# Expert loops of a two-layer mixture-of-experts kernel: the third product of each expert is issued behind the first two of the next

## What is computed

```
def run(args):
    xb, e = args
    return (jax.nn.silu(xb @ w1[e]) * (xb @ w3[e])) @ w2[e]
```

## Time and profile before

| | |
|---|---|
| median of 3 runs | 2323.3 us (2322.07 to 2324.07) |
| span of the profiled execution | 2330.8 us |
| PE busy | 2074.1 us (89%) |
| DVE, ACT, POOL busy | 787.4, 468.8, 189.3 us |
| moved in all | 640.95 MB, mean 275 GB/s |
| weight tiles of the experts | 192 of 2 MB |
| expert loop of layer 0, first product to last | 353.8 to 851.0 us |
| expert loop of layer 1, first product to last | 1095.4 to 1582.0 us |

### The profile page before, as it was taken

One profiled execution on the slowest core, in us unless ns is written; L12 is line 12 of the kernel. 1 busy time (PEld: TensorE's weight loads), 2 busy tenths in 40 slices (PEclk: granted clock), 3 DMA queues, 4 the chain that ended last, 5 costly groups with the idle time before them and its releaser, 6 DMA issues.

```text
span 2330.8 us, 30150 instructions
## 1 busy us (share of the span) xinstructions
PE 2074.1 (89%) x11971; PEld 1230.5 (53%) x11972; DVE 787.4 (34%) x1836; ACT 468.8 (20%) x1059; POOL 189.3 (8%) x240
## 2 busy tenths in 40 slices
PE   6998998889877889989877877798999999999998
PEld 4566475344444435757433433343775575775574
DVE  1355673111111116646111111114456413457413
ACT  2142112111111112411211111111123113123122
POOL 1000011111111110001111111111000000000000
PEclk9999999999999999979999999999999999999999
DMA  9236559999999993566999999997343233343230
GB/s 371 109 127 256 233 181 399 424 408 407 393 426 426 426 396 124 232 278 247 420 425 425 425 425 425 426 387 276 145 163 127 100 142 139 145 164 113 104 145 19
DMA packets 62872, 640.95 MB, mean 275 GB/s; under 512 B 15868, under 2 KB 16420, under 8 KB 24240
## 3 DMA queue, kind: packets, MB, share of 16 engines
q1 hardware_dynamic: 41728, 588.39, 61.4%
q0 software_dynamic: 19984, 44.74, 5.4%
q10 hardware_dynamic: 1056, 6.37, 0.7%
HBM read 622.50 MB, written 44.17 MB: 286 GB/s over the span
## 4 chain that ended last, share of the span: by engine, by line
PE 68%; DMA 21%; DVE 5%; ACT 3%; issue 2%; SPq 0%; POOL 0%; DVEq 0%; POOLq 0%; ACTq 0%
PE ps L854 17%; DMA ring<-in_moe 16%; PE ps L988 10%; PE ps L506 8%; PE ps L1002 6%; PE ps L1101 5%; PE ps L494 3%; PE ps L683 3%; PE ps L528 3%; PE ps L1173 2%; PE ps L860 2%; DMA ring<-in_denseA 2%; PE ps L759 2%; DVE scr L1767 2%; PE ps L857 1%
## 5 line engine op out<-in xcount | busy, mean ns | idle before, releaser
L854 PE MATMUL ps<-ring,scr 128*64 128x256 f32 (+1 forms) x4800 | 695.3, 445 | 102.2 <-DMA ring<-in_moe 53.4
L854 PEld LDWEIGHTS ps<-ring,scr 128*64 128x64 f32 x4800 | 348.2, 141 | 429.0 <-issue 170.2
L988 PE MATMUL ps<-ring,hT 128*128 128x512 f32 (+1 forms) x576 | 245.0, 577 | 2.0 <-ACT hT L1493 2.0
L1767 DVE TENSOR_TENSOR scr<-ps,scr 128x512 f32<-128x512 f32 (+3 forms) x98 | 54.7, 558 | 482.8 <-PE ps L854 401.5
L2429 DVE COPY scr<-ps 128x1024 f32<-128x1024 f32 x64 | 78.4, 1225 | 380.7 <-PE ps L854 345.7
L506 PE MATMUL ps<-ring,hT 128*128 128x512 f32 (+1 forms) x512 | 203.0, 555 | 4.1 <-ACT hT L1515 3.2
L1391 POOL DMA_INDIRECT ys_scratch<-scr,ytab x128 | 124.7, 974 | 838.2 <-DVE scr L2429 802.4
L988 PEld LDWEIGHTS ps<-ring,hT 128*128 128x128 f32 x576 | 107.3, 192 | 114.6 <-issue 109.5
L1463 ACT ACTIVATE scr<-ps 128x256 f32<-128x256 f32 (+2 forms) x168 | 71.3, 436 | 406.6 <-PE ps L494 406.5
L506 PEld LDWEIGHTS ps<-ring,hT 128*128 128x128 f32 x512 | 98.5, 195 | 98.9 <-issue 91.6
L1002 PE MATMUL ps<-hT,ring 128*128 128x256 f32 x640 | 145.5, 382 | 0.0
(11 more groups left out here) (331 smaller groups left out, 2059.6 us busy)
## 6 DMA issues: line engine op xcount, KB each, us to landing
ring<-in_moe SPq DMA_DIRECT2D x192, 2048.0 KB
ring<-in_denseB SPq DMA_DIRECT2D x48, 2048.0 KB
ring<-in_denseA SPq DMA_DIRECT2D x36, 2048.0 KB
scr<-ys_scratch POOLq DMA_DIRECT2D x6, 1024.0 KB, 7.6
modB<-mod_scratch POOLq DMA_DIRECT2D x10, 512.0 KB, 11.4
ring<-kv_scratch SPq DMA_DIRECT2D x2, 2048.0 KB
tok_scratch<-hb POOLq DMA_DIRECT2D x6, 512.0 KB, 2.9
memT_scratch<-modB ACTq DMA_DIRECT2D x2, 1024.0 KB, 6.7
```

The lines of the kernel that those rows point to most:

```text
L854: last = mm(out, lhs(c)[:, 0:64], w(c)[:, half * q:half * (q + 1)], start=(c == 0), stop=(c == n - 1))
L988: last = mm(T["open"][:, 0:cols], hT16[:, c, t * P:(t + 1) * P], w[:, c, 0:cols], start=(c == 0), stop=(c == DC - 1))
L1767: return V.tensor_tensor(out, a, b, op)
```

## The change

PE's function `expert` is taken apart into `up` (one of the first two products), `turn_gated` (the four transposes) and `down` (the third product). The new order is: first product of expert u, transposes of u - 1, second product of u, third product of u - 1. Each part has its own branch on narrow or wide. The third product of the last expert stands alone behind the loop. ACT and DVE follow the same order. SP loads the tiles in the new order (`place`, `in_order`, `tile_of`): w1 and w3 of expert 0, w1 and w3 of expert 1, w2 of expert 0, w1 and w3 of expert 2, w2 of expert 1, and so on. The two first products of an expert now lie in neighbouring banks (2p and 2p + 1), the output table moves from bank 3 to bank 7, the token blocks use banks 4 and 5 but for block 1 (2 and 3), and `down` waits by itself until the output before it is copied out.

```
+    def place(u, k):
+
+        if k == 2:
+            return 3 * u + 4 if u < E - 1 else 3 * E - 1
+        return 3 * u - 1 + k if u > 0 else k
+
...
-                released[baseM[l] + 3 * b + k] = (s, blocks_before[l] + b + 1)
+                released[baseM[l] + place(b, k)] = (s, blocks_before[l] + b + 1)
...
+            def up(i, u, k, flag):
...
+                def work(is_wide):
+                    w = moe_tile(i, G0 + (3 * u - 1 + k if u > 0 or type(i) is not int else k))
+                    products(2 * p + k, lambda c: w[:, c, :], DC, 512, lambda c: xgT[:, p, c, :],
+                             is_wide).then_inc((m_h1, m_h3)[k], 1)
...
+            def turn_gated(i, u, flag):
+
+                p = u % 2
+                pe.wait_ge(m_g, i * UNROLL + (B0 + u + 1))
...
+            def down(i, u, flag, q):
+
+                p = u % 2
+                pe.wait_ge(m_ge, i * UNROLL + (B0 + u + 1))
+                if B0 + u > 0 or type(i) is not int:
+                    pe.wait_ge(m_ye, i * UNROLL + (B0 + u))
...
+            now = flag_of(0, 0)
+            pe.wait_ge(m_xc, B0 + l + 1)
+            pe.wait_ge(cols_dve, l + 1)
+            up(0, 0, 0, now)
+            turn_block(1)
+            up(0, 0, 1, now)
+            output_table()
+            for u in range(1, UNROLL):
+                before, now = now, flag_of(0, u)
+                beside = blocks_beside(l, u)
+                pe.wait_ge(m_xc, B0 + l + u + 1)
+                up(0, u, 0, now)
+                turn_gated(0, u - 1, before)
+                up(0, u, 1, now)
...
+                if u == 1:
+                    pe.wait_ge(dest_ready, l + 1)
+                down(0, u - 1, before, G0 + 3 * u + 1)
...
             with pe.Fori(1, E // UNROLL) as i:
+                now = flag_of(i, -1)
                 for u in range(UNROLL):
-                    expert(u, i, False)
+                    before, now = now, flag_of(i, u)
+                    pe.wait_ge(m_xc, i * UNROLL + (B0 + l + u + 1))
+                    up(i, u, 0, now)
+                    turn_gated(i, u - 1, before)
+                    up(i, u, 1, now)
+                    down(i, u - 1, before, G0 + 3 * u + 1)
+            now = flag_of(0, E - 1)
+            turn_gated(0, E - 1, now)
+            down(0, E - 1, now, G0 + 3 * E - 1)
...
-            dense(lambda i: d["moe"][l][3 * EPG * (i // 3) + i % 3], 3 * UNROLL, G0)
+            dense(lambda i: d["moe"][l][tile_of(*in_order[i])], 3 * UNROLL - 1, G0)
...
-                    q = j - RING
-                    s = (m_h1, m_h3, m_y)[q % 3]
-                    sp_.wait_ge(s, i * UNROLL + (B0 + UNROLL + q // 3 + 1))
...
+                    m, k = divmod(j - RING, 3)
+                    sp_.wait_ge((m_h1, m_h3, m_y)[k], i * UNROLL + (B0 + UNROLL + m + (k < 2)))
...
+            dense(lambda i: d["moe"][l][tile_of(E - 1, 2)], 1, G0 + 3 * E - 1)
...
             with act.Fori(1, E // UNROLL) as i:
                 for u in range(UNROLL):
...
+                    silu_of(u % 2, i * UNROLL + (B0 + u))
+                    gated_out((u - 1) % 2, i * UNROLL + (B0 + u - 1))
+                    expert_tokens((u + 1) % 2, bass.ds(i * UNROLL + u + 1, 1), m_xc)
+            gated_out((E - 1) % 2, B0 + E - 1)
...
             for part in range(7):
                 table_part(part)
...
+                if part == 2:
+                    take_block(1)
...
             with dve.Fori(1, E // UNROLL) as i:
                 for u in range(UNROLL):
                     gated(u % 2, i * UNROLL + (B0 + u))
-                    outputs(u % 2, i * UNROLL + (B0 + u), i * 64 + (32 * ((B0 + u) // 2) + 16))
+                    outputs((u - 1) % 2, i * UNROLL + (B0 + u - 1), i * 64 + (32 * ((B0 + u - 1) // 2) + 16))
+            outputs_of(E - 1)
```

More of the change, by code:

```diff
@@ L414, in program, with tile_of @@
             for k, s in enumerate((m_h1, m_h3, m_y)):
-                released[baseM[l] + 3 * b + k] = (s, blocks_before[l] + b + 1)
+                released[baseM[l] + place(b, k)] = (s, blocks_before[l] + b + 1)
+    in_order = sorted(((u, k) for u in range(E) for k in range(3)), key=lambda at: place(*at))
+    def tile_of(u, k):
+        return 3 * (EPG * (u % NG) + u // NG) + k
     def blocks_beside(l, u):
@@ L422, in block_banks @@
     def block_banks(k):
[L424 to L425 removed]
+        return (2, 3) if k == 1 else (4, 5)
     def par_a(l):
@@ L831, in output_table @@
                 pe.wait_ge(tab_in, l + 1)
-                table = ps[:, 3, :]
+                table = ps[:, 7, :]
                 pairs = [(k, t) for k in range(2) for t in range(nt)]
@@ L863, in _ @@
             pe.wait_ge(plan_ready, l + 1)
-            def expert(u, i, peeled):
-                p = u % 2
[L869 to L903, removed]
@@ new lines, in moe_tile, with flag_of, either @@
+            def moe_tile(i, q):
+                pe.wait_ge(ring_full[q % RING], i * 48 + 16 * (q // RING + 1))
+                return ring[:, q % RING, :, :]
+            def flag_of(i, u):
+                return pe.value_load(wide[0:1, bass.ds(i * UNROLL + u, 1)], min_val=0, max_val=1)
+            def either(flag, work):
+                with pe.If(flag > 0):
+                    work(True)
+                with pe.Else():
+                    work(False)
+            def up(i, u, k, flag):
+                p = u % 2
+                def work(is_wide):
+                    w = moe_tile(i, G0 + (3 * u - 1 + k if u > 0 or type(i) is not int else k))
+                    products(2 * p + k, lambda c: w[:, c, :], DC, 512, lambda c: xgT[:, p, c, :],
+                             is_wide).then_inc((m_h1, m_h3)[k], 1)
+                either(flag, work)
@@ L904, in down, with work @@
+            def turn_gated(i, u, flag):
+                p = u % 2
+                pe.wait_ge(m_g, i * UNROLL + (B0 + u + 1))
+                def work(is_wide):
                     for c in range(4):
-                        bank, o = p + 2 * (c // 2), (c % 2) * P
-                        if flag:
+                        bank, o = 2 * p + c // 2, (c % 2) * P
+                        if is_wide:
                             last = nc.tensor.transpose(ps[:, bank, o:o + P],
@@ new lines, in down, with work @@
+            def down(i, u, flag, q):
[3 more added lines that the diff above has]
+                    pe.wait_ge(m_ye, i * UNROLL + (B0 + u))
+                def work(is_wide):
+                    w = moe_tile(i, q).rearrange("p (k n) x -> p k (n x)", n=2)
+                    products(6, lambda c: w[:, c, :], 4, D, lambda c: gT[:, p, c, :],
+                             is_wide).then_inc(m_y, 1)
+                either(flag, work)
@@ L1613, in _, with silu_of @@
             act.wait_ge(plan_ready, l + 1)
[L1614 to L1622, removed]
+            def silu_of(p, b):
+                act.wait_ge(m_h1, b + 1)
+                A(eb[:, p, :], ps[:, 2 * p, :], ACT.Silu).then_inc(m_e, 1)
+            silu_of(0, B0)
+            take_block(1)
+            blocks_taken(2)
+            expert_tokens(1, slice(1, 2), m_xc)
+            for u in range(1, UNROLL):
+                silu_of(u % 2, B0 + u)
+                gated_out((u - 1) % 2, B0 + u - 1)
+                beside = blocks_beside(l, u)
+                if beside:
+                    take_block(beside[0])
+                blocks_taken(min(u + 2, SLOT_BLOCKS[l]))
+                expert_tokens((u + 1) % 2, slice(u + 1, u + 2), m_xc)
+                if beside:
+                    take_block(beside[1])
+            blocks_taken(SLOT_BLOCKS[l])
             with act.Fori(1, E // UNROLL) as i:
                 for u in range(UNROLL):
[L1625 to L1631, removed]
+                    silu_of(u % 2, i * UNROLL + (B0 + u))
+                    gated_out((u - 1) % 2, i * UNROLL + (B0 + u - 1))
+                    expert_tokens((u + 1) % 2, bass.ds(i * UNROLL + u + 1, 1), m_xc)
+            gated_out((E - 1) % 2, B0 + E - 1)
             o = ov[l]
@@ L2436, in _, with outputs_of @@
                 table_part(part)
-            for u in range(UNROLL):
-                gated(u % 2, B0 + u)
[L2439 to L2444, removed]
+                if part == 2:
+                    take_block(1)
+            def outputs_of(u):
+                outputs(u % 2, B0 + u, 32 * ((B0 + u) // 2) + 16)
+            gated(0, B0)
+            rows_of_outputs()
+            for u in range(1, UNROLL):
+                gated(u % 2, B0 + u)
+                beside = blocks_beside(l, u)
+                if beside:
+                    take_block(beside[0])
+                outputs_of(u - 1)
+                if beside:
+                    take_block(beside[1])
+                if u == 2:
                     gate_values()
```

19 lines of the change are left out of this document (14 added, 5 removed).

## The result

| | before | changed |
|---|---|---|
| median of 6 runs, side by side | 2323.47 us (2322.07 to 2335.21) | 2309.24 us (2307.67 to 2312.99) |
| ratio, 95% interval | | 0.9939 (0.9921 to 0.9958) |
| profiled execution, span | 2330.8 us | 2308.0 us |
| PE busy | 2074.1 us | 2038.9 us |
| loop of layer 0, first product to first `MEM_V` product | 498.91 us | 489.91 us |

The kernel is faster by 14.2 us (0.6%). Forecast were 17.0 us and 2306.3 us. The line between loops and the rest is drawn at two rows of PE's timeline that both kernels have, the first product of expert 0 and the first `MEM_V` product (L968 before, L1006 now). Both loops are shorter, by 9.00 and 7.69 us.

A forecast was written before the change was run, and what follows sets the result against it. Tile loads bound narrow stretches; PE, stopping for DVE and ACT, bounds wide experts and layer 1's end. Gains 10.0 + 7.0 = 17.0 us, against the median 2306.3 us; forecast 2302 to 2311 us, outer range 2301 to 2314.

The forecast's parts named there:

- Layer 0, 10.0 us: Layer 0's expert loop: the time loads stood still would be gained, 9.7 us by bytes, 10.1 by the clock, taken as 10.0.
- The dips: Transfers around layer 0's wide experts, 450 to 650 us, at 403, 421, 409 and 388 GB/s; claimed to return near 426.
- the working with 9.4 and 10.6 us: Wide expert's second product: ends 9.4 us after its tile; the load needing its slot is due after 10.6 us: no gap.
- The way to the end: End of layer 0's loop: the first `MEM_V` product waits for its tile, so the 10.0 us reach the end.
- Layer 1, 8.0 us and 1.0 us back: Layer 1's end: last third product ends at 1574.0 instead of 1582.0 us; last rows under load return 1.0, leaving 7.0.
- The new wait of `down` at 0: Third product's wait for the previous output copy: no cost, since that copy ran an expert earlier.
- Start at 0: First four experts: table comes later, but loads behind 360 us are back to back; taken as 0, allowing 3.2 us either way.
- rival 3: PE's loop: added branches each cost time, at 1 us some 7 us more per group, about 2350 us; chance 0.05.
- Rival 2: Loads stand still as before: layer 0 gives nothing, layer 1 half of its 7 us, about 2320 us; chance 0.09.
- Rival 1: Only layer 0 pays: clock drop, longer last rows and start loss leave 11 us or less, about 2313 us; chance 0.16.
- The baseline: Whole kernel: 17.0 us off the profiled 2330.8 us gives 2313.8; that span is 7.5 us above the median, hence 2306.3.

The follow-up runs named there:

- experiment 5: The kernel before, with every expert told to PE as narrow, so the wide ones are computed for 64 columns only: 2305.89 us.
- experiment 6: The changed kernel, with every expert told to PE as narrow: 2416.54 us, with the path for overflowing tokens run in layer 1; layer 0's loop took 490.07 us.
- experiment 9: The changed kernel, with each layer's last third product in banks 4 and 5, not waiting for the output copy before it: 2312.41 us, one run.
- Experiment 8: The changed kernel, with every expert told to PE as wide: 2706.23 us.
- experiment 1: The kernel before, unchanged, profiled once more: 2332.48 us, span 2330.7 us.
- experiment 2: The changed kernel, unchanged, run once more: 2310.37 us against 2327.25 us for the kernel before, ratio 0.9935.
- experiment 7: The kernel before, with every expert told to PE as wide, computed for 128 columns: 2868.84 us.

## Why the forecast came out, step by step

**Layer 0, 10.0 us: right, 9.05 us measured.** The dips are gone and the gain is the time in which the loads stood still. From expert 6 to expert 19, 207.11 us of the earlier trace rows, it now takes 648.54 - 450.31 = 198.23 us on DVE's timeline, where 13 x 15.16 = 197.0 us had been named as due. Experiments 5 and 6 show that only the wide experts had held the loads up. The ring stayed busy across a wide expert, as the working with 9.4 and 10.6 us said. The way to the end was read wrong: in the changed kernel the first `MEM_V` product waits 1.68 us for DVE's copy of the last output (the row of 842.77 us), not for its tile; the repeat of the kernel before names that copy too. It costs next to nothing: in the changed kernel that copy ends at 842.38 us, and the tile, whose load went out at 825.57 us, lands at about 842.1 us (by the median of 16.5 us for such loads).

**Layer 1, 8.0 us and 1.0 us back: right, 7.4 us measured, 0.5 to 0.8 us back** (28.43 and 28.40 us from `MEM_V` to the transposes in two profiles, 27.88 and 27.66 us before). By experiment 5 most of it, 5.6 us, goes with the wide expert near the end. The working let the last third product start right behind its tile; the new wait put 0.5 us on that.

**What goes back in layer 0: missed.** The forecast let the first `MEM_V` product "and PE goes on from there" carry the 10 us to the end, with no price for layer 0. The price is 4.1 us in one profile and 2.0 us in the other. The forecast had seen that last rows under load take longer, and had charged it to layer 1 alone. But in layer 0 they had been under load before too (10.47 us); what changed is where the read falls against the next load, and that was not worked out. This is the term that makes 17.0 out of what is, by the profiles, 16.4 - 4.1 - 0.6 = 11.7 us or 16.4 - 2.0 - 0.7 = 13.7 us. The medians say 14.2 and 16.9 us, each with an interval several us wide. Taken off the median before, 2323.5 us, the profiles' 11.7 to 13.7 us give 2309.8 to 2311.8 us, the upper end of the forecast's 2302 to 2311 us. That a median came as near to 17.0 us as 16.9 is luck: no term of the forecast holds the difference.

**The new wait of `down` at 0: nearly right, for a wrong reason.** "That copy ran an expert earlier" holds in the loop, where no such wait is among PE's waits. It doesn't hold for the last expert, whose third product follows the one before it with only transposes between. There it costs 0.5 us in each layer (experiment 9), because a tile that lands at nearly the same time covers the rest.

**Start at 0: right within what can be told.** From 350 to 400 us the transfers have 406 GB/s after 399.

**Branches, rival 3: refuted.** Experiment 8 leaves no time for a jump, and the instruction queue has the 73 packets and 1.20 MB of the earlier trace rows. By the rule of the Trainium skill, "Runtime: NRT & Kernel Launch", section Instruction fetch mechanics, a taken branch stalls when its target lies outside the code already fetched; no run here shows such a stall, with twice as many branches as before.

**Rival 2, the loads stand still as before: refuted** by the four stretches at 426 GB/s. **Rival 1, only layer 0 pays: its parts are there,** in another place: last rows that wait longer, but behind layer 0. Its 2313 us lies above both medians, because layer 1 paid nearly in full.

**The baseline.** The forecast set its sum against the median and noted that the profiled execution was 7.5 us above it. That was needed: start and dense work between the loops took 568.96 and 568.45 us in the two profiles of the kernel before and 561.19 and 560.64 us in those of the changed one, but the order before had only 558.28 us in experiment 5. So about 8 of the profile's 22.8 us lie in work that the change hardly touches. Most of them go with the granted clock of the execution (experiments 1 and 2), and the order before can be without them (experiment 5). That the change has no part in them is not shown: both whole profiles of the kernel before have them, and neither of the changed kernel's does.

## What to carry to other kernels

Before taking a stop off an engine, find the stretches in which something else stands still because of it; here 112 us of stops went and 16 us came out of the loops, nearly all from stretches where the loads had run full, some 2 us from the last expert of layer 1. When the order of work changes, the order of the loads through a ring has to change with it, or the slot that is wanted first is the one that comes free last. And when a stage ends earlier, check what its last transfers now run beside: a read of output rows that meets a prefetch gave back 2 to 4 us.

## What was not expected of the hardware

The granted clock rose in the loops though PE was idle no less. The two loops, before and then after (length, busy PE, ..., clock, DMA share, GB/s):

```profile
353.77:852.68 498.91, 419.37 (x2680) 211.69 (x2681) 74.81 (x104) 81.04 (x143) 65.11 (x68) 0.96 0.99 417
1095.42:1583.79 488.37, 397.11 (x2696) 199.40 (x2697) 70.47 (x101) 78.37 (x135) 62.09 (x65) 0.95 1.00 419
```

```profile
352.86:842.77 489.91, 406.76 (x2680) 205.22 (x2681) 74.65 (x105) 75.18 (x143) 65.23 (x68) 0.99 1.01 425
1082.78:1563.46 480.68, 378.28 (x2696) 191.26 (x2697) 70.24 (x101) 72.44 (x135) 62.22 (x65) 0.99 1.01 424
```

PE is idle for 79.5 and 91.3 us before, for 83.2 and 102.4 us after. Yet a mean clock of 0.96 and 0.95 means, by estimate, about 40 and 49 us at 1.2 GHz (twice the missing share of the length), and 0.99 about 10 us in each loop. PE's busy time in the loops falls by 12.6 and 18.8 us with the same number of products. What differs is how the idle time lies: before, a stop for DVE, four short transposes and a stop for ACT in a row; after, single waits for a tile. That this is what sets the clock is argued, not shown. Where the loads are the bound, the higher clock saves nothing (experiments 5 and 6 have 0.96 and 0.99 at equal length); where PE is the bound, shorter products made some 58 of the 162.6 us (experiments 7 and 8). In the kernel itself PE was behind around the wide experts and at the end of layer 1, where the last third product takes 3.65 instead of 5.35 us; how much of the 16.4 us is the clock there was not separated.
